# Latent projections, retention and prompt attention interleaved in one stage

## The reference

```python
def layer_forward(x, pos, p, ret_s0, ret_chunk, attend):
    h = rmsnorm(x, p['norm_w'])
    z = h @ p['w_in']                                   # 1024 -> 3264 columns
    q_r, k_r, v_r, g_r, q_lat, c_raw, kpe_raw, g_a = jnp.split(z, _split_points(), axis=-1)
    q_r = apply_rope(q_r, cos_r, sin_r)
    k_r = apply_rope(k_r, cos_r, sin_r) * (RET_DK ** -0.5)
    o_r, s_new = retention_scan(q_r, k_r, v_r, ret_s0, ret_chunk)
    o_r = head_groupnorm(o_r, p['ret_gn_w']) * jax.nn.silu(g_r)
    q = rmsnorm(q_lat, p['q_a_norm_w']) @ p['w_qb']     # 384 -> 4 heads x (128 + 64)
    qn = rmsnorm(q[..., :MLA_NOPE], p['qn_w'])
    qp = apply_rope(rmsnorm(q[..., MLA_NOPE:], p['qp_w']), cos_a, sin_a)
    c = rmsnorm(c_raw, p['kv_a_norm_w'])                # 256 columns
    kpe = apply_rope(rmsnorm(kpe_raw, p['kp_w']), cos_a, sin_a)
    o_a = attend(qn, qp, c, kpe, p) * jax.nn.silu(g_a)  # kn = rmsnorm(c @ w_kb), v = c @ w_vb
    y = jnp.concatenate([o_r, o_a], axis=-1) @ p['w_out']
    return x + y, c, kpe, s_new
```

## Time and profile before

| | us |
|---|---|
| median of 3 runs | 1434.77 |
| the 3 runs | 1434.35 to 1437.07 |
| the profiled execution | 1435.2 |
| its span on the core | 1433.1 |
| PE busy (matmuls) | 1280.2, 89% |
| DVE busy | 733.5, 51% |
| ACT busy | 531.8, 37% |
| POOL busy | 431.8, 30% |
| mean granted TensorE clock | 0.947 of full speed |

### The profile page before, as it was taken

The page is one execution under the profiler, slowest core; times in us unless marked ns, Lnnn a source line. Parts: engine busy times, 40 slices in busy tenths (PEclk is TensorE's granted clock), DMA queues, the critical chain, the costliest instruction groups (busy, mean ns, idle before and its releaser), DMA issues.

```text
span 1433.1 us, 26883 instructions
## 1 busy us (share of the span) xinstructions
PE 1280.2 (89%) x8624; PEld 1161.9 (81%) x8624; DVE 733.5 (51%) x1392; ACT 531.8 (37%) x1382; POOL 431.8 (30%) x592
## 2 busy tenths in 40 slices
PE   5999988677999999978869999877879999999798
PEld 4999964556999999968859999545669999999588
DVE  4423256576466665554244223475765655566442
ACT  4312225232555555533042112242325555555230
POOL 1000143353445445430010002333525444444300
PEclk9999999699999999988979999996999999999889
DMA  9422030012362222202514120300123632222035
GB/s 308 134 94 93 0 80 1 1 30 66 98 183 75 77 79 79 74 7 98 186 53 139 49 93 0 80 1 1 39 65 94 180 84 79 77 74 74 1 110 177
DMA packets 132774, 115.85 MB, mean 81 GB/s; under 512 B 46513, under 2 KB 127346, under 8 KB 132658
## 3 DMA queue, kind: packets, MB, share of 16 engines
q1 hardware_dynamic: 132658, 114.52, 26.5%
HBM read 103.57 MB, written 13.27 MB: 82 GB/s over the span
## 4 chain that ended last, share of the span: by engine, by line
issue 50%; POOL 19%; PE 16%; POOLq 7%; DVE 5%; ACT 2%; DVEq 1%; DMA 0%; SPq 0%; ACTq 0%
POOL krs L1869 14%; POOL rstat L1758 3%; POOLq L1863 2%; POOLq L1865 2%; PE ps L540 2%; PE ps L541 2%; PE ps L542 2%; POOLq L1753 2%; PE ps L883 1%; PE ps L912 1%; DVE mx L1548 1%; PE ps L549 1%; PE ps L548 1%; PE ps L721 1%; PE ps L696 1%
## 5 line engine op out<-in xcount | busy, mean ns | idle before, releaser
L1613 DVE TENSOR_REDUCE kss<-ksq 128x8 f32<-128x1024 f32 x128 | 156.0, 1219 | 217.2 <-ACT ksq L1222 217.2
L540 PE MATMUL ps<-w_hi,hT_hi 128*128 128x408 f32 (+2 forms) x704 | 244.0, 347 | 0.0
L541 PE MATMUL ps<-w_lo,hT_hi 128*128 128x408 f32 (+2 forms) x704 | 241.9, 344 | 0.0
L542 PE MATMUL ps<-w_hi,hT_lo 128*128 128x408 f32 (+2 forms) x704 | 241.2, 343 | 0.0
L1222 ACT ACTIVATE ksq<-ps 128x544 f32<-128x544 f32 x256 | 159.9, 625 | 200.3 <-PE ps L883 200.3
L883 PE MATMUL ps<-wq_hi,cT_hi 128*128 128x272 f32 x1024 | 223.7, 300 | 0.0
L1869 POOL TENSOR_TENSOR krs<-kss_t,cst 128x8 f32<-128x8 f32 x128 | 209.2, 1634 | 19.1 <-DVE Ssc L1627 2.5
L883 PE MATMUL ps<-wq_lo,cT_hi 128*128 128x272 f32 x1024 | 212.5, 289 | 0.0
L883 PE MATMUL ps<-wq_hi,cT_lo 128*128 128x272 f32 x1024 | 212.4, 289 | 0.0
L1752 POOL TENSOR_SCALAR pool_tmp<-stat 128x1 f32<-128x1 f32 (+2 forms) x70 | 18.3, 261 | 480.9 <-ACT ps L1055 297.7
L883 PEld LDWEIGHTS ps<-wq_lo,cT_hi 128*128 128x128 f32 x1024 | 162.0, 190 | 0.0
(11 more groups left out here) (196 smaller groups left out, 2063.2 us busy)
## 6 DMA issues: line engine op xcount, KB each, us to landing
ckv<-in_cache_ckv SPq DMA_DIRECT2D x256, 128.0 KB, 2.0
raw<-in_w_in SPq DMA_DIRECT2D x68, 408.0 KB, 4.1
kp<-in_cache_kpe SPq DMA_DIRECT2D x256, 32.0 KB, 1.8
raw<-in_w_out SPq DMA_DIRECT2D x16, 340.0 KB, 3.9
S<-in_state_ret SPq DMA_DIRECT2D x8, 512.0 KB, 6.0
out<-S SPq DMA_DIRECT2D x8, 512.0 KB, 3.2
z<-out SPq DMA_DIRECT2D x2, 2048.0 KB, 8.6
wqb<-in_w_qb SPq DMA_DIRECT2D x3, 1152.0 KB, 9.2
```

Of the source, the lines that this page charges most:

```text
L540: pe.matmul(out, a_hi, b_hi, start=first, stop=False)
L541: pe.matmul(out, a_hi, b_lo, start=False, stop=False)
L542: return pe.matmul(out, a_lo, b_hi, start=False, stop=last)
L1613: dve.tensor_reduce(kss[:, hs, 2 * k:2 * k + 2, :], ksq[:, q % 2, :, c0:c0 + HW].rearrange("p j (h k) -> p j h k", h=H), AX.X, ALU.add).th ...
```

## The change

Stages 2 and 3 become one stage, with all semaphore counts for stages lowered by one. In it:

- PE's order is written out anew (below), as are those of ACT, DVE and POOL.
- PSUM: latents and queries share banks 0 and 1, values and then keys share bank 2. Scores of block n go to bank 3 + n % 2 and so does the output of that block, so scores of block n+1 wait for DVE's output of block n-1 (`po_ok`). Turned probabilities use bank 5. Retention has banks 6 and 7 for all that had banks 0 to 3, so a tile's `ret_turn` waits for the `ret_norm` of the one before.
- `attn_step(n)` on PE is: attend block n-1, turn the probabilities of block n, scores of block n+1. On DVE: output of block n-1, maximum of block n+1.
- The sample state is updated for all four heads early, the updates with 32 rows instead of 64, and POOL's `step_mask` makes half as many elements.
- Each tile's queries `qnT`, `qpT` and latents `cT` are kept for two tiles instead of all.
- Absorbing the key weights and the scores of the new tokens lie between the last attention blocks.
- SP loads all four quarters of the first sequence's pages when the key weights are absorbed, then stores the prompt's state.

The rotation of the retention queries and keys, their decay, the retention gates and the split of `wkb` move into the input projection, where they are done in place in `z`. The copy `ks` goes. The loops over groups in the input projection are written out.

Core of the diff (new order of PE and DVE in the joint stage, and what is new in the input projection):

```diff
+            def scores(n):
+                i, h = divmod(n, H)
...
+                if n >= 2:
+                    pe.wait_ge(po_ok, n - 1)
...
             def attn_step(n):
+                if n >= 1:
+                    attend(n - 1)
+                if n < NBLK:
+                    turn_probs(n)
                 if n + 1 < NBLK:
                     scores(n + 1)
-                if n < NBLK:
-                    turn_probs(n)
-                if n >= 1:
-                    attend(n - 1)
...
+            latents(0)
+            turn_wkb()
+            v_project(0)
+            q_project(0)
+            k_project(0)
+            ret_turn(0)
+            ret_scores(0)
+            k_turn(0)
+            step_read()
+            q_turn(0)
+            latents(1)
+            ret_out(0)
+            v_project(1)
+            q_project(1)
+            scores(0)
+            k_project(1)
+            step_update(0)
+            attn_step(0)
+            step_update(1)
+
+            for t in range(2, TILES):
+                n0 = 4 * t - 7
+                k_turn(t - 1)
+                attn_step(n0)
+                q_turn(t - 1)
+                if t == 2:
...
+                else:
+                    ret_turn(t - 1)
+                    latents(t)
+                    attn_step(n0 + 1)
+                    ret_scores(t - 1)
+                    if t < S_TILE:
+                        v_project(t)
+                    q_project(t)
+                attn_step(n0 + 2)
+                ret_out(t - 1)
+                k_project(t)
+                attn_step(n0 + 3)
+            attn_step(13)
+            q_turn(S_TILE)
+            ret_turn(S_TILE)
+            attn_step(14)
+            absorb()
+            ret_scores(S_TILE)
+            attn_step(15)
+            ret_out(S_TILE)
+            new_scores()
+            attn_step(16)
+            stage_end(pe, 1)
...
# DVE, input projection
+            split(4, 0)
+            rope_tiles(0, 1)
+            keep_z(3)
+            split(5, 1)
+            rope_tiles(2, 3)
+            keep_z(4)
+            split(6, 0)
+            rope_tiles(S_TILE)
...
+            keep_z(5)
+            split(7, 1)
+            for t in range(TILES):
+                gates_r(t)
+            keep_z(6)
...
# DVE, joint stage
+            gates(0)
+            sum_q(0)
+            sum_k(0)
+            scale_k(0)
+            scale_q(0)
+            ret_mask(0)
+            gates(1)
+            ret_state(0)
+            sum_q(1)
+            ret_norm(0)
+            attn_max(0)
+            sum_k(1)
+            scale_q(1)
+            step_add(0)
+            attn_step(0)
+            scale_k(1)
+            step_add(1)
+
+            for t in range(2, TILES):
+                n0 = 4 * t - 7
+                attn_step(n0)
...
+                    attn_step(n0 + 1)
+                    ret_mask(t - 1)
+                sum_q(t)
...
+                attn_step(n0 + 2)
+                scale_q(t)
+                ret_state(t - 1)
+                sum_k(t)
+                gates(t)
+                attn_step(n0 + 3)
+                ret_norm(t - 1)
+                if t < S_TILE:
+                    scale_k(t)
```

More of the change, by code:

```diff
@@ L601, in _ @@
             group(1, 1, False)
-            with pe.Fori(1, NG // 2) as i:
-                group(i * 2, 0, False)
-                group(i * 2 + 1, 1, False)
+            for g in range(2, NG):
+                group(g, g % 2, False)
             stage_end(pe, 0)
[L608 to L615, removed]
             def latents(t):
@@ new lines, in rope_mix_qk, with rope_tiles @@
+            def rope_mix_qk(t):
+                n = rows(t)
+                t1, t2 = rope_t(t)
+                dve.wait_ge(rope2, t + 1)
+                q = z[0:n, t, 0:2 * HW].rearrange("p (h a k) -> p h a k", h=2 * H, a=2)
+                dve.tensor_tensor(q[:, :, 0, :], t1[:, :, 0, :], t2[:, :, 1, :], ALU.subtract)
+                dve.tensor_tensor(q[:, :, 1, :], t1[:, :, 1, :], t2[:, :, 0, :], ALU.add).then_inc(rope_mix, 1)
+            def rope_tiles(*tiles):
+                dve.drain()
+                for t in tiles:
+                    rope_cos(t)
+                dve.drain()
+                for t in tiles:
+                    rope_mix_qk(t)
+                dve.drain()
@@ new lines, in gates_r @@
+            def gates_r(t):
+                n = rows(t)
+                dve.wait_ge(gr_tanh, t + 1)
+                dve.scalar_tensor_tensor(out=zc(t, C_GR, HW), in0=gate_r[0:n, t % 2, :],
+                                         scalar=1.0, in1=zc(t, C_GR, HW), op0=ALU.add, op1=ALU.mult)
+                dve.drain()
+                dve.tensor_tensor(zc(t, C_GR, HW), zc(t, C_GR, HW), gn_b[0:n, :], ALU.mult).then_inc(gr_ok, 1)
+            keep_z(0)
+            split(2, 0)
+            keep_z(1)
@@ new lines, in _ @@
+            scale_k(1)
+            step_add(1)
+            for t in range(2, TILES):
+                n0 = 4 * t - 7
+                attn_step(n0)
+                if t == 2:
+                    step_add(2)
+                    step_add(3)
+                    attn_step(n0 + 1)
+                else:
+                    attn_step(n0 + 1)
+                    ret_mask(t - 1)
+                sum_q(t)
+                if t == 2:
+                    ret_mask(1)
+                attn_step(n0 + 2)
+                scale_q(t)
+                ret_state(t - 1)
+                sum_k(t)
+                gates(t)
+                attn_step(n0 + 3)
+                ret_norm(t - 1)
+                if t < S_TILE:
+                    scale_k(t)
@@ L1590, in _ @@
+            attn_step(13)
+            attn_step(14)
+            ret_mask(S_TILE)
+            split_absorbed()
+            attn_step(15)
+            ret_state(S_TILE)
+            new_scores()
+            ret_norm(S_TILE)
+            attn_step(16)
+            stage_end(dve, 1)
             for b in range(2):
```

743 lines of the change are left out of this document (377 added, 366 removed).

## The result

The changed kernel takes 1476.5 us, the median of 4 runs (1474.7 to 1480.2), against 1435.6 us (1434.4 to 1437.1) for the kernel before on the same chip: a ratio of 1.0285, 95% interval 1.0267 to 1.0303. The forecast was 1474, with a range of 1410 to 1505. The profiled execution has a span of 1472.8 us against 1433.1, and the 39.7 us between them lie in the joint stage alone: measured from PE's first work of the stage to PE's first work of stage 4, it takes 179.90 and 180.06 us in the two layers, against 159.27 and 161.09 for stages 2 and 3, 39.6 us more.

A forecast was written before the change was run, and what follows sets the result against it. PE was taken as busiest before, PE and DVE as taking turns after; 180 us a layer against 159.3 and 161.1 added 39.6 to the profiled 1435.2, 1474.8, with the median 0.4 lower: 1474, range 1410 to 1505.

The forecast's parts named there:

- Input projection at nothing: Input projection: moved rotations and gates fit DVE's 14.3 us free in a group, costing nothing (bounds 0 to about 3 us a layer).
- The new wait decides: Joint stage: scores of block n+1 wait for block n-1's output on DVE, so PE and DVE take turns, 34 us a period.
- The sign of being wrong: Joint stage: PE idle below 69 us over both layers, or a period near 27 us, would refute the forecast.
- The holes: PE's idle gaps in each joint-stage period: 4.3 us before the fourth scores, 3.2 us more before k_turn.
- The stage: Joint stage per layer: start 47, three periods of 34 and tail 22 give 171 us, plus 9 for the clock: 180.
- The start: Joint stage until k_turn(1): 47 us at full clock, with 5 us more if the half clock lasts.
- The clock's terms: Joint stage: half clock after idle gaps costs 5 us at the start and 1.3 in each of three periods, 9 together.
- Stage 4 at nothing: Stage 4: SP's reordered page loads and state store cost nothing; at worst it starts 3 us later.
- Holes filled: Rival for the joint stage: interleaving fills PE's holes, 135 us a layer, so 1385 us; chance 0.08.
- The period of 27 us: Rival: joint-stage period stays at 27 us with start and tail as forecast, 150 us a layer, so 1414; chance 0.13.
- at 30 us the layers come out even: Joint stage: a period under about 30 us means a gain, 30 us no change; chance of even 0.05.
- The full loss of the clock: Rival: the clock falls fully in every joint-stage period and again in the start, 195 us a layer, so 1505; chance 0.22.

The follow-up runs named there:

- e10: The changed kernel with outputs in the turned probabilities' bank, gates and ret_norm behind scale_k on DVE, and unread transposes in PE's holes: 1418.9 us, 0.989 of before.

## Why the prediction was right

**The account.** From before to the moved work alone: -16. From there to the joint stage with a bank that scores need not share: 1420.1 to 1434.5, +14. From there to the change as it is: +42. The three parts give +40, with +41 measured. So the interleaving by itself loses, the shared bank with its order is the most of it, and the moved work is a gain that the other two hide. DVE's order and filling don't turn this round: the joint stage with both is at 1418.9 us, the stages apart with filling at 1402.1.

**By the prediction's steps.**
- Input projection at nothing: right. The groups stay at 21.00 us, and PE's first work of the joint stage comes at 193.64 us (194.48 before).
- "The new wait decides": shown. Its removal won 42 us; in the waits, 21.2 us of a stage are that line. The sign of being wrong (PE without a matmul for less than 69 us over both layers) did not come: it is 96.9.
- The holes: 4.3 us before the fourth scores were forecast, 4.37 and 4.03 measured; 3.2 before `k_turn`, 3.05 and 3.17. Both, worked out from DVE's lines at the prices of before, were good to 0.3 us. A third hole, of 2.19 and 2.08 us before the third scores, is not in the prediction.
- The stage: 180 us, 179.90 and 180.06 measured. That they agree so closely is luck. The start was to be 47 + 5 = 52 us and took 47.94: 4.1 too much. Two periods were to be 35.3 each and took 36.83 and 36.05, and the third with the tail 35.3 + 22 = 57.3, and took 59.08: together 4.1 too little.
- The clock's terms are the ones that were mis-sized, with the right sum. In the start 5 us were put down. Filling its hole won 0.7 from the first `k_turn` to the second (31.23 us for 31.91), though the clock still fell once behind it, so the full price there was not measured. In a period it was 1.3, by a choice for which the prediction's own reason (half of what follows the hole is waited for anyway) does not quite give the number. Filling won 1.1 and 3.2, and 4.1 in the third period and tail (35.76, 32.86, 54.97). So 9.1 in all against the 9 of the sum. In the second period and behind the third `k_turn`, which ran at 1.00 when filled, the time at full clock was 1.1 and 1.0 us under the working (34 and 56), and the clock's part 1.9 and 2.8 over it.
- Stage 4 at nothing: right. All that lies outside the stages in question takes 1112.8 us against 1112.7.

**The rivals.** "Holes filled" (1385) misread what binds: even with the bank free PE and DVE wait for each other at `scale_k`. The period of 27 us (1414) was not reached; 29.5 was the best without filling (28.0 once with it, in e10), and at 29.5 the kernel stood at 1432, just under before, as "at 30 us the layers come out even" had it. The full loss of the clock (1505) did not come: every period has its fall, but little of it costs time. By the mean clock of 0.83 some 61 us of a stage lie at half speed ((1 - 0.83) x 179.9 / 0.5, an estimate), by that of the filled kernel, 0.95, some 17; and these 44 us fewer won 9.1. The Trainium skill, "TensorE: Matmul & The Clock Gate", section "HAM oscillation", describes such a fall in every round; the trace agrees in kind, with 0.50 behind the holes before `k_turn` and the fourth scores; behind those of 2.19 and 2.08 us before the third scores the clock stayed at 1.00.

What the change could not have done otherwise with eight banks is open in part. The Trainium skill, "PSUM — Partial Sum Buffer", section "PSUM bank collisions raise a hardware error", asks for PSUM to be guarded by bank and group of 32 partitions, and not by address. Scores and outputs both fill all 128 partitions, so separate columns of the scores' bank are no way out by it; no run here shows such a collision. Of the two places tried for the output, bank 5 cost less by 42 us.

**Where my theories of the experiments fell.** I set "the bank" and "DVE's order" against each other and priced both at 3 to 4 us a period. The bank was worth 18 and 21 us a layer. The order was worth 3.5 and 3.7 by itself and 4.5 and 3.0 with the bank free, counted from the first `k_turn`, about what had been put down for a single period. The mistake was to price a wait by the work that it stops hiding: the run that shares the bank in the kernel apart shows as much again behind it, and in the joint stage each delay returned through the other engine and the clock.

## What to carry to other kernels

Before two stages are joined, count the banks: if the joined stage makes an output share a bank with the next block's scores, price the whole chain behind the new wait (scores, maximum, exponential, turned probabilities), not the score alone, and look for another tenant of a bank, as here the turned probabilities. Take the parts of a change apart: its gain of 16 us was real and stood alone. Where PE has holes that can't be closed, look at the granted clock behind them, and if what follows is dense, filling them with transposes that nobody reads can be a cheap gain (18 us here, or 1.1% by the kernel before beside each run).

## What the runs showed of the hardware

I had not expected idle work to be worth so much. In four pairs it won 21.8 us (1476.5 to 1454.7), 5.5 (1434.5 to 1428.9), 13.1 (1432.0 to 1418.9) and 18.0 (1420.1 to 1402.1); the last two pairs have some 30 transposes at the end of the stage as well. By the kernel before beside each run it is 1.4, 0.2, 0.8 and 1.1% of the time. In the third pair the two joint stages are 7.5 us shorter, and 7.2 us of the profile's gain lie outside them, part of it where the filled end lets stage 4 start at full clock. In this pair, shown here without and then with filling, the first windows of stage 4 go from 0.54 and 0.60 to 1.00:

```profile
351.46:355.46 4.00, 2.74 (x13) 2.34 (x14) 1.11 (x5) 1.30 (x4) 0.00 (x0) 0.54 0.30 83
355.46:359.46 4.00, 4.00 (x23) 4.00 (x22) 0.69 (x1) 0.94 (x4) 0.00 (x0) 0.60 0.48 107
```

```profile
348.93:352.93 4.00, 2.63 (x21) 2.40 (x22) 1.66 (x6) 1.53 (x4) 0.00 (x0) 1.00 0.47 119
352.93:356.93 4.00, 4.00 (x36) 4.00 (x35) 1.54 (x3) 2.20 (x7) 0.03 (x1) 1.00 0.40 101
```
